# A hybrid decoder layer: gating at the head of its slot, a copy on ScalarE, halved residual additions, an own order for the last tile, no meta queries, the last reciprocal a step sooner

## The reference

```python
hn = rms_norm(h, norm_gain)
c_q, c_kv, k_idx, w_idx, z_attn, q_g, k_g, v_g, z_g, b_g, a_g = split(hn @ w_in)
# group A, 8 heads x 64: queries from a 256-wide latent, keys and values from a 128-wide one, QK-norm,
# an indexer picks the top 256 causal keys of each query, softmax over these with a relative bias
o_attn = dsa(c_q, c_kv, k_idx, w_idx, ...) * silu(z_attn)
# group B, 4 heads x 128: gated DeltaNet on conv(q), conv(k), conv(v), a scan over chunks
v_new = u - w @ S
o     = q_dec @ S + aqk @ v_new
S     = S * chunk_decay + k_dec.T @ v_new
o_gdn = rms_norm(o, g_out) * silu(z_g)
y = concat([o_attn, o_gdn]) @ w_out
return (h + y)[:, 16:]          # the meta tokens' rows are dropped
```

## Time and profile before

| | before |
|---|---|
| median of 3 runs | 870.71 us (870.37 to 872.8) |
| the profiled execution | 870.25 us |
| its span, first to last instruction | 868.5 us |
| mean granted clock of TensorE | 0.985 |
| busy: PE, PEld, DVE, ACT, POOL | 812.1, 486.3, 610.5, 387.5, 251.9 us |

### The profile page before, as it was taken

One profiled execution on the slowest core, in us unless ns is written; L12 is line 12 of the kernel. 1 busy time (PEld: TensorE's weight loads), 2 busy tenths in 40 slices (PEclk: granted clock), 3 DMA queues, 4 the chain that ended last, 5 costly groups with the idle time before them and its releaser, 6 DMA issues.

```text
span 868.5 us, 16529 instructions
## 1 busy us (share of the span) xinstructions
PE 812.1 (94%) x6357; PEld 486.3 (56%) x6357; DVE 610.5 (70%) x1409; ACT 387.5 (45%) x1234; POOL 251.9 (29%) x254
## 2 busy tenths in 40 slices
PE   6999899999999999999959999999799889889897
PEld 2554434444446666666626667766666556556554
DVE  2444789999999999999665567766576565566441
ACT  3443756777792555545435455665222022022010
POOL 8000100000000646577543432264333223223210
PEclk9999999999999999999989999999799999999999
DMA  6252201030003011000100201103421121112011
GB/s 174 70 206 97 74 15 35 24 122 37 24 23 112 1 50 48 2 1 0 50 23 2 97 26 55 59 26 124 158 75 52 48 98 60 64 50 74 33 44 49
DMA packets 29363, 51.72 MB, mean 60 GB/s; under 512 B 3668, under 2 KB 11204, under 8 KB 29284
## 3 DMA queue, kind: packets, MB, share of 16 engines
q1 hardware_dynamic: 28740, 50.55, 17.4%
q0 software_dynamic: 544, 0.10, 0.3%
HBM read 40.11 MB, written 12.10 MB: 60 GB/s over the span
## 4 chain that ended last, share of the span: by engine, by line
PE 80%; DVE 11%; ACT 4%; issue 2%; DMA 1%; SPq 1%; DVEq 0%; ACTq 0%
PE ps L1668 19%; PE ps L1646 11%; PE ps L1876 11%; PE ps L1523 6%; PE ps L1717 5%; PE ps L1706 4%; PE ps L1688 4%; DVE areaQ L1318 2%; PE ps L1620 2%; PE ps L1780 2%; PE ps L1574 1%; DVE tmp L1450 1%; PE ps L1618 1%; PE ps L1855 1%; PE ps L1752 1%
## 5 line engine op out<-in xcount | busy, mean ns | idle before, releaser
L1185 DVE TENSOR_SCALAR_CACHE_REDUCE junk<-scores,iw 128x272 bf16<-128x272 f32 (+6 forms) x224 | 213.6, 954 | 8.2
L1668 PE MATMUL ps<-areaH,areaW 128*128 128x384 f32 (+1 forms) x576 | 168.1, 455 | 1.6 <-ACT areaQ L924 1.6
L1668 PEld LDWEIGHTS ps<-areaH,areaW 128*128 128x128 f32 x576 | 109.4, 190 | 59.9 <-issue 1.8
L736 POOL TENSOR_TENSOR staging<-staging,areaC 128x520 f32<-128x520 f32 x60 | 88.4, 1507 | 63.2 <-ACT areaC L962 63.2
L750 POOL TENSOR_TENSOR areaH<-areaQ,masks 128x512 f32<-128x512 f32 x37 | 45.3, 1230 | 101.4 <-PE ps L1800 93.5
L1876 PE MATMUL ps<-areaW,scores 128*128 128x512 f32 x128 | 58.8, 604 | 8.0 <-DVE scores L1446 8.0
L783 POOL TENSOR_TENSOR areaW<-scores,tmp 128x256 f32<-128x256 f32 (+1 forms) x64 | 44.6, 724 | 62.9 <-DVE small L1271 52.8
L1523 PE MATMUL ps<-areaW,areaH 128*128 128x460 f32 (+1 forms) x144 | 59.8, 571 | 1.7 <-DVE areaH L1107 1.6
L962 ACT ACTIVATE areaC<-areaC,small 128x520 f32<-128x520 f32 x60 | 42.5, 723 | 32.7 <-POOL staging L736 32.7
L1646 PE MATMUL ps<-areaH,areaW 128*128 128x512 f32 x128 | 56.3, 594 | 0.0
L1646 PE MATMUL ps<-areaW,areaH 128*128 128x512 f32 x128 | 56.2, 592 | 0.0
(11 more groups left out here) (272 smaller groups left out, 1432.4 us busy)
## 6 DMA issues: line engine op xcount, KB each, us to landing
areaW<-in_w_in SPq DMA_DIRECT2D x5, 2048.0 KB, 8.0
areaH<-row_factor_scratch SPq DMA_DIRECT2D x18, 256.0 KB, 4.7
areaC<-in_x SPq DMA_DIRECT2D x8, 512.0 KB, 3.6
tmp<-in_x SPq DMA_DIRECT2D x8, 512.0 KB, 4.8
y<-tmp SPq DMA_DIRECT2D x8, 512.0 KB, 3.7
areaW<-in_w_out SPq DMA_DIRECT2D x3, 768.0 KB, 5.6
gate_a_scratch<-staging SPq DMA_DIRECT2D x8, 256.0 KB, 2.3
gate_g_scratch<-staging SPq DMA_DIRECT2D x8, 256.0 KB, 2.0
```

The source lines that it names most:

```text
L736: nc.gpsimd.tensor_tensor(sums, sums, prod, ALU.add).then_inc(s_cvP, 1)
L1185: tlink(V.tensor_scalar(junk[:, 0:n], scores[:, SC0[i]:SC0[i] + n], at, init, op, ALU.add, accum_out=cnt[:, i - 1:i]))
L1668: ins = mm(ps[:, n % 4, 0:hi - lo], wslot[:, g % 2, k, 128 * m:128 * m + 128], hT[:, k, lo:hi], start=k == 0, stop=k == KD - 1)
```

## The change

- `g` moves to the head of its slot, ahead of the youngest tile's stage, and `yt` ahead of `p2`.
- `c`, the copy of the turned tile out of its bank, is done by ScalarE, after the `x` copies of its slot.
- `fin` is two stages, `f0` (512 columns, after p5) and `f1` (after p7). p0 waits for the tile before's `f0`, p2 for its `f1`.
- The last 14 slots are written out by hand (`RUN_DOWN`): tile 7's p4 to p7 lie between tile 8's stages, tile 8's state product and state update aren't made, and tile 8's result is stored in two halves.
- Tile 0's queries aren't computed: two products and 8 of 16 heads in `norm_kq(0)` go.
- The reciprocal of the last attention block is taken in step 32 instead of 33, after a wait for all of its sums. The others stay: the old condition gives steps 5, 9, ..., 33, the new one 5, 9, ..., 29 and 32.

```diff
-REC_AT = [(["v"], []), ([], ["os"]), (["p0"], []), (["p1"], ["g"]), (["p2"], ["yt", "ks"]), (["p3"], ["c"]),
-          (["p4", "p5"], []), (["p6", "p7", "fin"], [])]
+REC_AT = [(["v"], []), ([], ["os"]), (["p0"], []), (["g", "p1"], []), (["yt", "p2"], ["ks"]), (["c", "p3"], []),
+          (["p4", "p5", "f0"], []), (["p6", "p7", "f1"], [])]
+LAST_TILE, BEFORE = NT - 1, NT - 2
+RUN_DOWN = [[(LAST_TILE, "x64"), (BEFORE, "p4")], [(LAST_TILE, "y64"), (BEFORE, "p5"), (BEFORE, "f0")],
+            [(LAST_TILE, "v"), (BEFORE, "p6")], [(LAST_TILE, "os"), (BEFORE, "p7"), (BEFORE, "f1")],
+            [(LAST_TILE, "g"), (LAST_TILE, "p0")], [(LAST_TILE, "yt"), (LAST_TILE, "p1"), (LAST_TILE, "c")]] + [
+            [(LAST_TILE, stage)] for stage in ("p2", "p3", "p4", "p5", "f0", "p6", "p7", "f1")]
...
-    for slot in range(RECUR[NT - 1] + len(REC_AT)):
+    for slot in range(FIRST[LAST_TILE] + pre_list(LAST_TILE).index("x64")):
...
-    return slots
+    return slots + RUN_DOWN
...
             def store(t):
                 u = t - 1
+                if t == NT - 1:
+                    sp.wait_ge(g_dve, DV(t, "out0"))
+                    sp.dma_start(out[0, 128 * u:128 * u + 128, 0:512], xres[u % 2][:, 0:512]).then_inc(s_out[u % 2], 16)
+                    sp.wait_ge(g_dve, DV(t, "out"))
+                    sp.dma_start(out[0, 128 * u:128 * u + 128, 512:D], xres[u % 2][:, 512:D]).then_inc(s_out[u % 2], 16)
+                    return
...
             def norm_kq(t):
-                n = ROWS[t]
+                n, nh = ROWS[t], 16 if t else 8
...
-                for h in range(16):
+                for h in range(nh):
...
+                    if stage == "c":
+                        act.wait_ge(g_pe, PE(t, "yt"))
+                        nc.scalar.copy(yT, heads(5)).then_inc(g_act, 1)
...
-                    elif stage == "c":
-                        dve.wait_ge(g_pe, PE(t, "yt"))
-                        V.tensor_copy(yT, bank(5)).then_inc(g_dve, 1)
-                    elif stage == "fin":
-                        dve.wait_ge(g_pe, PE(t, "out"))
+                    elif stage in ("f0", "f1"):
+                        half_ = int(stage[1])
+                        part = slice(512 * half_, 512 * half_ + 512)
+                        dve.wait_ge(g_pe, PE(t, "out" if half_ else "out0"))
                         dve.wait_ge(s_xr[u % 2], 16 * (u // 2 + 1))
-                        V.tensor_tensor(xres[u % 2], pf[:, 3072:4096], xres[u % 2], ALU.add).then_inc(g_dve, 1)
+                        V.tensor_tensor(xres[u % 2][:, part], ps[:, 6 + half_, :], xres[u % 2][:, part],
+                                        ALU.add).then_inc(g_dve, 1)
...
-                if LAG <= step < NP + LAG and (step - LAG) % HP == HP - 1:
+                if LAG <= step < NP and (step - LAG) % HP == HP - 1 or step == NP:
                     i = (step - LAG) // HP
                     dve.wait_ge(s_P, HA * (i + 1))
                     V.reciprocal(rinv[:, i % 2, :], rs[:, HA * i:HA * i + HA]).then_inc(s_ri, 1)
...
-                for k in range(2):
+                for k in range(2 if t else 0):
                     mm(ps[0:n, 1, :], cT[:, k, tok(t)], wuq[:, k, :], start=k == 0, stop=k == 1)
...
-                                pe.wait_ge(g_dve, DV(t - 1, "yt"))
+                                pe.wait_ge(g_act, AC(t - 1, "yt"))
...
-                        for h in range(HG):
+                        for h in range(HG if t < NT - 1 else 0):
                             ins = mm(col(4, h), kdec[r_][0:n, h, :], vnew[0:n, h, :], start=True, stop=True)
-                        ins.then_inc(g_pe, 1)
+                        if t < NT - 1:
+                            ins.then_inc(g_pe, 1)
...
                             if t > 1:
-                                pe.wait_ge(g_dve, DV(t - 1, "out"))
+                                pe.wait_ge(g_dve, DV(t - 1, "out0"))
+                        if stage == "p2" and t > 1:
+                            pe.wait_ge(g_dve, DV(t - 1, "out"))
                         if stage == "p4":
-                            pe.wait_ge(g_dve, DV(t, "yt"))
+                            pe.wait_ge(g_act, AC(t, "yt"))
...
-                        if q == 7:
+                        if q in (5, 7):
                             ins.then_inc(g_pe, 1)
```

More of the change, by code:

```diff
@@ L134, in slot_list @@
         slots.append(order)
-    return slots
+    return slots + RUN_DOWN
 def pe_steps(t, stage):
-    return {"nat": ["kn", "vn"], "os": ["o", "s"] if t else ["s"], "p7": ["out"],
-            "fin": [], "c": [], "g": [], "rb": []}.get(stage, [] if stage[0] == "p" else [stage])
+    return {"nat": ["kn", "vn"], "os": ["o"] * (t > 0) + ["s"] * (t < NT - 1), "p5": ["out0"], "p7": ["out"],
+            "f0": [], "f1": [], "c": [], "g": [], "rb": []}.get(stage, [] if stage[0] == "p" else [stage])
 def dve_steps(t, stage):
@@ L150, in dve_steps @@
             "kk": ["at", "aq"], "cc": ["t1", "tc1", "ttc1", "ttf1"], "v": ["vnew"],
-            "os": ["s0", "s1", "s2", "s"] if t else ["s"], "g": ["y0", "y1", "y2", "y"], "c": ["yt"],
-            "fin": ["out"]}.get(stage, [])
+            "os": (["s0", "s1", "s2", "s"] if t else ["s"]) if t < NT - 1 else [], "g": ["y0", "y1", "y2", "y"],
+            "f0": ["out0"], "f1": ["out"]}.get(stage, [])
 def act_steps(t, stage):
@@ L157, in act_steps @@
         return [stage]
-    return {"rb": [f"{g}{h}" for g in ("ga", "gq") for h in range(4)] + (["eq"] if t else []),
+    return {"rb": [f"{g}{h}" for g in ("ga", "gq") for h in range(4)] + (["eq"] if t else []), "c": ["yt"],
             "os": ["so0", "so1", "so2", "so3", "ln", "ro"] if t else []}.get(stage, [])
@@ L658, in _ @@
             store(NB)
-            for q in s_out:
-                sp.wait_ge(q, 16 * (NB // 2))
+            sp.wait_ge(s_out[0], 16 * (NB // 2))
+            sp.wait_ge(s_out[1], 16 * (NB // 2 + 1))
         @block.gpsimd
@@ L901, in norm_kq @@
                 nc.scalar.preload_act_table_set("natural_log_exp_and_others")
-                link(A(rk[0:n, t % 2, :], ssk[0:n, t % 2, :], ACT.Ln, bias=epst[0:n]))
-                link(A(rk[0:n, t % 2, :], rk[0:n, t % 2, :], ACT.Exp, scale=-0.5))
+                link(A(rk[0:n, t % 2, 0:nh], ssk[0:n, t % 2, 0:nh], ACT.Ln, bias=epst[0:n]))
+                link(A(rk[0:n, t % 2, 0:nh], rk[0:n, t % 2, 0:nh], ACT.Exp, scale=-0.5))
                 if t >= 2:
                     act.wait_ge(s_kqT, t - 1)
-                for h in range(16):
+                for h in range(nh):
                     ins = A(qkn[0:n, t % 2, 64 * h:64 * h + 64], pf[0:n, 64 * h:64 * h + 64], ACT.Copy,
@@ L1437, in recurrent @@
                         V.tensor_copy(vnew[0:ROWS[t]], bank(4)[0:ROWS[t]]).then_inc(g_dve, 1)
-                    elif stage == "os":
+                    elif stage == "os" and t < NT - 1:
                         state(t)
```

## The result

The changed kernel takes 860.16 us as a median of 4 runs (856.33 to 863.24), the kernel before on the same chip 871.1: a ratio of 0.987, 95% interval 0.9825 to 0.9914, so 1.3% faster. The forecast was 858.1 in a range of 853.5 to 862.5. The profiled execution took 861.26 us with a span of 859.5, against 870.25 and 868.5.

The account below looks back on a forecast made before the run. TensorE was taken as the bound, 80% of the chain of work that ended last. Gains of 5.6 + 0.4 + 3.1 + 1.2 + 2.3 = 12.6 us off 870.25 gave 857.65, as a median 858.1, range 853.5 to 862.5.

Parts of the forecast that it names:

- Full tiles: Tiles 2 to 6: halved addition, copy on ScalarE and moved gating save 1.12 us per tile, 5.6 over five periods.
- The rival that gating is the new bound: Full tiles: VectorE reaches gating later than L1364's place, each tile gains only 0.45 us; 861.5 us, chance 0.16.
- its own terms: Full tile sum: 0.45 + 1.48 + 0.73 - 1.54 us, TensorE's old wait ahead of yt becoming a longer one.
- Reciprocals: End of attention: last reciprocal a step sooner removes TensorE's 2.26 us wait; kk ends at 613.0, 3.1 us sooner.
- the second stretch at 1.2 GHz: Between 622 and 628 us, TensorE's clock halved: costs about 3.9 us and was left in place.
- The rival had the stretch going away: The slow-clock stretch at 622 to 628 us vanishes as well, another 3.9 us: 854.2 us, chance 0.13.
- the 857.65 of the sum: Whole kernel: profiled 870.25 us less 12.6 us of summed gains; as a median 858.1.
- Meta queries: Tile 0's turn: two 512-column products dropped, 1.8 us at full clock, of which 1.2 was taken to arrive.
- VectorE's taps would catch up half of it: Near 430 us, last convolution taps wait only 0.91 us, so 0.9 of the dropped products' 1.8 us might arrive.
- Last tile: Kernel's end: own order, TensorE 1.15 us sooner, half addition 0.54, smaller last store 0.6; together 2.3 us (1.3 to 3.2).
- The p stages that run alone: Kernel's end: each takes 1.88 us alone instead of 1.76 in a run of four, costing 0.57 us.
- the estimate: Last store, half as large: saves between nothing and 1.3 us, the middle 0.6 taken.

Follow-up runs that it names:

- the two other orders: Changed kernel with p2 ahead of yt, gating still at its slot's head: 853.25 us; changed kernel with gating and yt at their old places: 854.31 us.
- the expectation for the kernel before: Kernel before the change plus seven unused products in TensorE's waits between tile 1's y32 and tile 2's y4: 868.97 us, ratio 0.9967.

## Why the prediction was right, and where it wasn't

**Full tiles.** The step held: forecast 1.12 per tile, measured 1.11 in four of the five periods and 0.84 in the first (33.05 to 32.21), which makes 5.32 instead of 5.6. The wait ahead of yt was 1.38 by its bracket and 1.54 from start to start, as forecast; that ahead of y8 fell from 0.61 to 0.39, and from p7's end to y8 it is 2.33 us instead of 2.74, 0.41 less (0.45). The rival that gating is the new bound was ruled out by its place: it starts where L1364 stood. What the prediction didn't say is that the move was a loss by itself: its own terms had it (0.73 becomes 1.54), and the two other orders confirm it with 0.85 and 1.34 us per tile.

**Reciprocals.** Right by its mechanism and its size: kk ends at 613.01 us (forecast 613.0), and 2.98 of 3.1 us reach p0 of tile 1 where the clock holds. The term that was wrong is the one behind it: the second stretch at 1.2 GHz was "left as it was", at some 3.9 us, as if it had one price. It cost 2.4 in the profile of the kernel before, and between 1.9 and 5.6 in five profiles of the changed code. The profiled execution is one of the two long ones, and so it shows 0.16 us lost from the values product to p0 where three other profiles of the same code show 2.9, 2.9 and 3.6 gained against the same profile of the kernel before. The rival had the stretch going away, with a chance of 0.13: it is there in all eight profiles without fillers. It comes without any single wait above 0.9 us, and 1664 columns of filler took it away in five of six profiles and shortened it to 3.4 us in the sixth (the expectation for the kernel before put their number at 2.4 thousand, which is a miscount). What makes it short in one execution and long in the next isn't shown.

**The spread.** The changed kernel's four runs, ordered by mean granted clock 0.976, 0.980, 0.982 and 0.986, took 863.24, 861.26, 859.06 and 856.33 us. The fastest is 1.3 us below the 857.65 of the sum and the slowest 5.6 above. The forecast was good for runs with the clock of the profiled execution before (0.985); three of the four had a lower one, which fits the median's 2 us more. A right total was in part luck: 1.1 us more than forecast came from the last tile, and the part ahead of tile 1 swings by 5 us from one execution to the next.

**Meta queries.** 1.72 for the forecast's 1.8 at 112 us. The argument that VectorE's taps would catch up half of it was wrong: 319.13 us pass with and without. The reason given for the 2.75 us of the earlier trace rows, a clock that rose meanwhile, is right, but the changed kernel's profile has no fall there that could pass on to successors. What is left of the 1.72 at the end isn't shown: behind 430 us the executions differ by as much.

**Last tile.** 3.35 instead of 2.3, by two terms. The p stages that run alone were charged 0.57 from their durations, 1.88 against 1.76. From start to start four of them take 1.91, 1.82, 1.72 and 1.72, in all 7.17, and the two pairs of before 3.63 and 3.54, also 7.17: the term is zero, the duration only holds the overlap with the next. A small one stands in its place: the last tile's yt begins 1.98 us after p0 and not 1.72, so it waits some 0.26 for its gating. And y8 of the last tile gains its 0.41 too, a sixth time, which I had counted five times. TensorE's rows for this, and the last two stores of the changed kernel (KB each, us to landing):

```profile
839.92 1.88 PE L1893 MATMUL ps<-areaW,scores 128*128 128x512 f32 x4
841.64 1.88 PE L1893 MATMUL ps<-areaW,areaQ 128*128 128x512 f32 x4
843.62 0.66 PE L1875 MATMUL ps<-small,areaH 128*128 128x128 f32 x4
```

```profile
y<-tmp SPq DMA_DIRECT2D x2, 256.0 KB, 2.0
```

The store fits the estimate: from the issue to the end of the span 2.45 us (857.05 to 859.5) against 3.05 (865.45 to 868.5), 0.60 less for half the bytes. The landing shrank by as much, from 2.6 to 2.0; in proportion to the bytes it would have been by 1.3. The Trainium skill's rate of 436 GB/s (DMA: Bandwidth & Descriptors, Anatomy of one DMA) gives 0.60 for 256 KB, an estimate with which the trace agrees. The fixed 2.0 us stand there for DMAs issued by GpSimd, and not for every DMA as the prediction has it: these stores are issued by SyncE, and by the same rate 1.4 us of their landing times are fixed, an estimate too.

## What to carry to other kernels

When an edit puts a producer and its consumer both earlier, ask what stood between them: here p2 had covered the gating, and putting it back was worth 1.34 us per tile on top of all other edits. Read the granted clock over every sparse stretch next to an edit as a term of the sum of its own, with a bound on both sides, for it can take back as much as the edit gives, and look at several executions of the same code before you put its length down to the edit; a few unused products in the waits there tell what the clock costs, and may be worth keeping. Cost a matmul by the distance from its start to the next start, not by its duration.

## What the hardware showed that I had not expected

- Unused work made the kernel faster: with seven more products kk to p0 of tile 1 took 18.13 us where the same code without them took 20.00 to 23.74, and the kernel before gained 2.4.
- A wait of 2.59 us inside dense work halved the clock in four of five tiles and not in the fifth, so the same wait costs some 1.6 us of clock or none. The clock also fell with no wait above 0.9 us in this case, where the products are small, and once (p2 ahead of yt, at 604 us) with none above 0.55 in the 13 us before.
- Kernels that share their code up to 604 us differ there by up to 3.5 us from one execution to the next, with the same instructions ahead of it. For terms below that, only distances between marks in a profile tell anything.
